# Two transformer blocks on one core: first norm by ones and logarithm, two modulation scales on TensorE, head 0's forget gate first, pool evictions ahead of weight splits

## The reference

```python
def first_block(x, c, norm_pre_w, ada_w, ada_b, w_in, ...):
    silu_c = silu(c)
    mod = silu_c @ ada_w + ada_b                 # 1024 -> 3072
    shift, scale, gate = split(mod, 3)
    h = rms_norm(x, norm_pre_w) * (1 + scale) + shift
    u_pool, g_pool, q, f_pre, i_in, g_h = split(h @ w_in, 6)   # 1024 each
    pool_out = multiscale_pool(u_pool, pool_w, pool_scale) * silu(g_pool)
    f = lb + (1 - lb) * sigmoid(f_pre)
    log_f = log(f); k = 1 - f                    # 8 heads of 128, chunks of 64
    o = hgrn2_chunkwise(q, log_f, k, i_in)
    o = rms_norm(o, hgrn_norm_w) * silu(g_h)
    y = concatenate([pool_out, o]) @ w_out
    return x + gate * rms_norm(y, norm_post_w)

def second_block(x, c, ctx, c_ctx, w_ada, b_ada, w_in, ...):
    x = layer_norm(x); ctx = layer_norm(ctx)
    mod = silu(c) @ w_ada + b_ada                # 1024 -> 6144
    ...                                          # latent attention, convolution, FFN
```

## Time and profile before

| | us |
|---|---|
| median of 3 runs | 1217.19 |
| profiled execution, its own time | 1213.69 |
| its span in the trace | 1211.9 |
| PE busy | 1133.1 (94%) |
| DVE busy | 860.9 (71%) |
| ACT busy | 550.8 (45%) |
| POOL (GpSimd) busy | 165.3 (14%) |

### The profile page before, as it was taken

How to read it: one execution, slowest core, us unless ns; L and a number is a source line. 1 busy time by engine, 2 the same in 40 slices (tenths; PEclk the granted TensorE clock), 3 DMA queues, 4 the chain that set the end, 5 groups by cost and what they waited for, 6 DMA issues and landing times.

```text
span 1211.9 us, 14076 instructions
## 1 busy us (share of the span) xinstructions
PE 1133.1 (94%) x5488; PEld 925.6 (76%) x5488; DVE 860.9 (71%) x1352; ACT 550.8 (45%) x851; POOL 165.3 (14%) x179
## 2 busy tenths in 40 slices
PE   1879999999999989989999999998999999999996
PEld 0667888888888868879887766777888888888885
DVE  5868899988876775455888899586666565655236
ACT  3266454545433242667334656545634434342230
POOL 0034433344424210001010010000000000000001
PEclk9989999999999999999999999999999999999999
DMA  7724133233344567472211011111322222234201
GB/s 295 296 106 154 70 140 139 74 136 132 111 148 165 182 220 171 178 66 84 96 50 47 1 70 45 60 56 49 104 105 104 105 76 99 104 115 173 80 33 69
DMA packets 28306, 136.59 MB, mean 113 GB/s; under 512 B 7760, under 2 KB 8016, under 8 KB 14416
## 3 DMA queue, kind: packets, MB, share of 16 engines
q1 hardware_dynamic: 20448, 128.46, 30.5%
q10 hardware_dynamic: 7792, 7.24, 2.4%
HBM read 133.57 MB, written 2.12 MB: 112 GB/s over the span
## 4 chain that ended last, share of the span: by engine, by line
PE 64%; DVE 18%; ACT 9%; DMA 4%; issue 3%; POOL 1%; ACTq 0%; DVEq 0%; SPq 0%
PE PB L185 63%; DVE RAW L1365 4%; ACT WH L199 3%; DMA RAW<-in_wstream 2%; ACT L200 2%; DVE WL L206 2%; DVE CV L214 2%; DVE XL L214 1%; DVE SS L214 1%; DMA vectors<-PX 1%; DVE HL L206 1%; DMA XL<-in_xT 1%; DVE HB L231 1%; PE PB L193 1%; POOL UPA L206 1%
## 5 line engine op out<-in xcount | busy, mean ns | idle before, releaser
L185 PE MATMUL PB<-HH,WH 128*128 128x512 f32 (+1 forms) x896 | 353.3, 394 | 18.5 <-DVE WL L206 8.0
L206 DVE TENSOR_TENSOR WL<-RAW,WH 128x1024 fp32r<-128x1024 f32 (+2 forms) x174 | 202.5, 1171 | 199.1 <-ACT WH L199 198.4
L185 PE MATMUL PB<-HH,WL 128*128 128x512 f32 (+1 forms) x896 | 342.7, 382 | 0.0
L185 PE MATMUL PB<-HL,WH 128*128 128x512 f32 (+1 forms) x896 | 342.4, 382 | 0.0
L199 ACT ACTIVATE WH<-RAW 128x1024 fp32r<-128x1024 f32 (+2 forms) x174 | 169.6, 981 | 296.5 <-PE PB L185 262.5
L185 PEld LDWEIGHTS PB<-HH,WH 128*128 128x128 f32 x896 | 171.1, 191 | 54.0 <-DVE WL L206 9.0
L185 PEld LDWEIGHTS PB<-HH,WL 128*128 128x128 f32 x896 | 170.7, 190 | 33.3
L185 PEld LDWEIGHTS PB<-HL,WH 128*128 128x128 f32 x896 | 171.2, 191 | 29.0 <-issue 0.5
L214 DVE SCALAR_TENSOR_TENSOR CV<-VP,PC,CV 128x512 f32<-128x512 f32 x120 | 86.7, 765 | 0.7
L206 POOL TENSOR_TENSOR PX<-PX,NPOW 128x2 f32<-128x2 f32 (+2 forms) x7 | 6.2, 893 | 482.0 <-DVE PX L206 436.1
L185 PE MATMUL PB<-WH,AH 128*128 128x512 f32 x176 | 68.5, 389 | 0.0
(11 more groups left out here) (270 smaller groups left out, 1851.9 us busy)
## 6 DMA issues: line engine op xcount, KB each, us to landing
RAW<-in_wstream SPq DMA_DIRECT2D x108, 1024.0 KB, 4.8
RAW<-in_wstream SPq DMA_DIRECT2D x5, 768.0 KB, 4.3
RAW<-in_wstream SPq DMA_DIRECT2D x5, 512.0 KB, 3.6
XL<-in_xT SPq DMA_DIRECT2D x2, 1024.0 KB, 8.2
HB<-in_x SPq DMA_DIRECT2D x2, 1024.0 KB, 6.3
out<-XL SPq DMA_DIRECT2D x8, 256.0 KB, 2.0
ROWS<-in_rows ACTq DMA_DIRECT2D x3, 512.0 KB, 7.7
XC<-in_ctx SPq DMA_DIRECT2D x1, 1024.0 KB, 7.1
```

What stands on the lines that cost most here:

```text
L185: return self.put(lambda e: e.matmul(o, l, r, start=start, stop=stop, skip_group_check=skip))
L206: return self.put(lambda e: e.tensor_tensor(o, a, b, op))
```

## The change

It makes these edits. The lengths of the stream's items stay as they are; one copy of c in columns (8) is added to the parameters.

1. c's row is loaded first on ACT's queue, its Silu comes before the squares, and c also stands in the parameters as columns.
2. The squares are summed in pairs on DVE and by three matmuls with all of `ONES` (512 columns each) on PE; ACT takes logarithm and exponential (-0.5) from PSUM to `Q0`. The power, the diagonals, the spread and the sum for `BX` go; the exponential for the lower bounds and its four small operations move behind the start.
3. The scale tiles of pairs 1 and 2 become items of kind "m", laid out for PE: 16 fp32 matmuls of one column each (`modulation`). They stand on PE before the first tiles and before the fifth.
4. Of head 0 the forget gate's block comes first in the last pair, and sigmoid, f, logarithm, k and scan of head 0 stand ahead of the other evictions and between the splits. Both dots of the first later item stand there too; the others of the plan stay where they are or move up, and in blocks 6, 10, 14, ... 30 they stand on ticks 2 and 3.
5. In `pool_mix` the eviction and both parts come ahead of the split of block nb+4.
6. The squares of x for the second block's layer norm are four dots of DVE in blocks 65 and 66.
7. The split of block 74 comes ahead of the last `y_squares` and `gated`.

```diff
 def stream_layout():
-    first = [("a", "ada_w", j + b) for j in range(0, 8, 2) for b in (8, 0)]
+    first = [("m" if b and j in (2, 4) else "a", "ada_w", j + b) for j in range(0, 8, 2) for b in (8, 0)]
 def dot_plan():
-    todo = [(n, i, vec) for n in LATER_ADA for i, vec in dots_of(n)]
+    todo = [(n, i, vec) for n in LATER_ADA[1:] for i, vec in dots_of(n)]
     for n, t in ticks:
-        if t % 2 and todo:
+        if (t >= 2 if n < B_POOL and n % 4 == 2 else t % 2) and todo:
 # sp_prog, fetch
+                elif LAY[n - NRAW][0] == "m":
+                    sp.wait_ge(S_.p_sm, ("mod", (LAY[n - NRAW][2] - 8) // 2))
 # pool_prog
-        g.wait_ge(S_.v_ax, "xs")
-        power(sct(2)[:, 4:8], sct(2)[:, 0:4], 4, "xpow")
 # act_prog, start
+        a.dma(ROW["c"], A["rows"][:, 0:D]).then_inc(S_.cs, "c", by=16)
         a.dma(PC[:, :], A["params"][:, :]).then_inc(S_.par, "par", by=16)
...
+        a.wait_ge(S_.cs, "c")
+        a.act(ROW["c"], ROW["c"], ACTF.Silu).then_inc(S_.a_s, "c")
         a.wait_ge(S_.par, "par")
-        a.dma(ROW["c"], A["rows"][:, 0:D]).then_inc(S_.cs, "c", by=16)
-        a.act(LT, LT, ACTF.Exp).then_inc(S_.a_s, "lt")
+        a.act(col("c", 0, 8), col("c", 0, 8), ACTF.Silu).then_inc(S_.a_s, "ccol")
         for k in range(8):
             a.act(XSQ[k], XT[:, k, :], ACTF.Square).then_inc(S_.a_s, ("xsq", k))
+        a.act(Q0[:, :], aux.of("xs"), ACTF.Ln, bias=NPOW[:, 7:8], scale=1.0 / D).then_inc(S_.a_ax, "xs")
+        a.act(Q0[:, :], Q0[:, :], ACTF.Exp, scale=-0.5).then_inc(S_.a_s, "xd")
+        a.act(LT, LT, ACTF.Exp).then_inc(S_.a_s, "lt")
 # act_prog, head 0
-        for b in range(4):
-            split(b + NW)
-        for b in range(3):
-            head(0, b)
+        a.wait_ge(S_.p_blk, 1)
+        a.act(Kb, main.of(("z", 0, 1)), ACTF.Sigmoid).then_inc(S_.a_ev, ("z", 0, 1))
+        split(NW)
+        a.wait_ge(S_.v_s, ("f", 0))
+        a.act(XR[3], Kb, ACTF.Ln).then_inc(S_.a_s, ("ln", 0))
+        head(0, 0)
+        split(NW + 1)
+        head(0, 2)
+        split(NW + 2)
+        split(NW + 3)
 # act_prog, pool_mix (DVE alike)
-            after(nb)
             kk = 2 * p + m
             mix(kk, GPS[p % 2][:, m, :], (S_.v_ev if p else S_.v_ax, ("pm", p, m)), None if kk >= 2 else (S_.p_blk, 53))
+            split(nb + NW)
 # act_prog, seam (DVE alike, ahead of gated(3, 1))
         shifted(1)
+        split(B_IN2 + 2)
         y_squares(2, 1)
 # dve_prog, start
-        for k in range(1, 8):
+        for k in (1, 2, 3):
             v.tt(Q0[:, :], Q0[:, :], XSQ[k], ADD).then_inc(S_.v_s, ("xs", k))
-        v.ts(BX, aux.of("xs")[:, 0:4], 1.0 / D, EPS2, MUL, ADD)
-        v.ts(sct(2)[:, 0:4], aux.of("xs")[:, 0:4], 1.0 / D, EPS1, MUL, ADD).then_inc(S_.v_ax, "xs")
-        diag(DG, sct(2)[:, 4:8], 4, "xd")
+        for k in (4, 6):
+            v.tt(XSQ[k], XSQ[k], XSQ[k + 1], ADD).then_inc(S_.v_s, ("xs", k))
         for p in range(4):
...
+            if p in FIRST_MOD:
+                v.wait_ge(S_.p_sm, ("mod", p))
+                v.tt(M1[:, 8 + 2 * p:10 + 2 * p], aux.of(("mod", p))[:, 0:2], col("ada_b", 8 + 2 * p, 2), ADD)\
+                    .then_inc(S_.v_ax, ("mod", p))
...
-                v.stt(XT[:, k, :], XT[:, k, :], A1[:, k:k + 1], aux.of("xd"), MUL, MUL)\
-                    .then_inc(S_.v_s, ("u", k), *["xd"] * (k == 7))
+                v.stt(XT[:, k, :], XT[:, k, :], A1[:, k:k + 1], Q0[:, :], MUL, MUL).then_inc(S_.v_s, ("u", k))
 # dve_prog, head 0: OML, LT, LB, OML (moved here), then
+        dot(first, 0, "c")
+        v.ts(Kb, Kb, OML[:, 0:1], LB[:, 0:1], MUL, ADD).then_inc(S_.v_s, ("f", 0))
+        split(NW)
+        dot(first, 1, "c")
+        v.ts(Kb, Kb, -1.0, 1.0, MUL, ADD).then_inc(S_.v_s, ("k", 0))
+        v.scan(Bb, SM[:, :], XR[3]).then_inc(S_.v_s, ("b", 0))
+        for n in (1, 2, 3):
+            split(NW + n)
 # dve_prog, blocks 65 and 66
+                for i in ((0, 1) if nb == B_OUT + 11 else (2, 3)):
+                    v.dot(XSQ2, XT2[:, i, :], XT2[:, i, :], MUL, BX[:, i:i + 1], scale=1.0 / D).then_inc(S_.v_st, ("bx", i))
 # pe_prog
-        sums(bk, Q0, 4, 0).then_inc(S_.p_sm, "xs")
-        spread("xd", DG, 4, "xd")
+        for n, k in enumerate((3, 4, 6)):
+            pe.wait_ge(S_.v_s, ("xs", k))
+            op = pe.mm(bk, ONES[:, :], XSQ[k] if n else Q0[:, :], n == 0, n == 2)
+        op.then_inc(S_.p_sm, "xs")
+        def modulation(p):
+            n = FIRST_MOD[p]
+            bk = take_aux(("mod", p), 1 + p)
+            pe.wait_ge(S_.raw[n % NRAW], n)
+            pe.wait_ge(S_.a_s, "ccol")
+            for i in range(2):
+                for k in range(8):
+                    op = pe.mm(bk[:, i:i + 1], raw_of(n)[:, D * i + 128 * k:D * i + 128 * k + 128], col("c", k), k == 0, k == 7)
+            op.then_inc(S_.p_sm, ("mod", p))
+        modulation(1)
...
         for b in range(2):
             for k in range(2):
                 first_tile(b, k)
+        modulation(2)
...
-        for p in (2, 3):
-            for b in range(4):
+        for p, bs in ((2, range(4)), (3, (1, 0, 2, 3))):
+            for b in bs:
```

More of the change, by code:

```diff
@@ L268 @@
 for n_, it_ in enumerate(LAY):
-    if it_[0] == "a":
+    if it_[0] in ("a", "m"):
         size_ = 2048
@@ L279 @@
 NRAW, NW = 3, 4
+FIRST_MOD = {(it[2] - 8) // 2: n for n, it in enumerate(LAY) if it[0] == "m"}
 FIRST_ADA = [n for n, it in enumerate(LAY) if it[0] == "a" and it[1] == "ada_w" and it[2] < 16]
@@ L856, in act_prog @@
             a.act(XSQ[k], XT[:, k, :], ACTF.Square).then_inc(S_.a_s, ("xsq", k))
-        a.wait_ge(S_.cs, "c")
-        a.act(ROW["c"], ROW["c"], ACTF.Silu).then_inc(S_.a_s, "c")
+        a.wait_ge(S_.p_sm, "xs")
+        a.wait_ge(S_.g_s, "npow")
+        a.act(Q0[:, :], aux.of("xs"), ACTF.Ln, bias=NPOW[:, 7:8], scale=1.0 / D).then_inc(S_.a_ax, "xs")
+        a.wait_ge(S_.a_ax, "xs")
+        a.act(Q0[:, :], Q0[:, :], ACTF.Exp, scale=-0.5).then_inc(S_.a_s, "xd")
+        a.wait_ge(S_.v_s, "lt")
+        a.act(LT, LT, ACTF.Exp).then_inc(S_.a_s, "lt")
         def h_high(k):
@@ L1398, in dve_prog @@
             v.tt(Q0[:, :], Q0[:, :], XSQ[k], ADD).then_inc(S_.v_s, ("xs", k))
-        v.wait_ge(S_.p_sm, "xs")
-        v.ts(BX, aux.of("xs")[:, 0:4], 1.0 / D, EPS2, MUL, ADD)
-        v.ts(sct(2)[:, 0:4], aux.of("xs")[:, 0:4], 1.0 / D, EPS1, MUL, ADD).then_inc(S_.v_ax, "xs")
-        v.wait_ge(S_.g_s, "xpow")
-        v.wait_ge(S_.idn, "idn")
-        diag(DG, sct(2)[:, 4:8], 4, "xd")
+        for k in (4, 6):
+            v.wait_ge(S_.a_s, ("xsq", k + 1))
+            v.tt(XSQ[k], XSQ[k], XSQ[k + 1], ADD).then_inc(S_.v_s, ("xs", k))
         for p in range(4):
-            for n in FIRST_ADA[2 * p:2 * p + 2]:
-                for i, vec in dots_of(n):
-                    dot(n, i, vec)
+            for n in FIRST_ADA:
+                if LAY[n][2] % 8 == 2 * p:
+                    for i, vec in dots_of(n):
+                        dot(n, i, vec)
             ks = slice(2 * p, 2 * p + 2)
+            if p in FIRST_MOD:
+                v.wait_ge(S_.p_sm, ("mod", p))
+                v.tt(M1[:, 8 + 2 * p:10 + 2 * p], aux.of(("mod", p))[:, 0:2], col("ada_b", 8 + 2 * p, 2), ADD)\
+                    .then_inc(S_.v_ax, ("mod", p))
+                v.wait_ge(S_.v_ax, ("mod", p))
             v.wait_ge(S_.v_ada, ("ada_w", 2 * p + 1, "c"))
@@ L1504, in hgrn @@
                     .then_inc(S_.v_ax, ("dg", h))
-        for b in range(4):
-            split(b + NW)
-        for b in range(4):
-            head(0, b)
+        v.wait_ge(S_.a_s, "lt")
+        v.recip(OML, LT).then_inc(S_.v_s)
+        v.wait_ge(S_.v_s)
+        v.tt(LT, LT, OML, MUL).then_inc(S_.v_s)
+        v.wait_ge(S_.v_s)
+        v.tt(LB, LT, LT, SUB).then_inc(S_.v_s)
+        v.wait_ge(S_.v_s)
+        v.ts(OML, LB, -1.0, 1.0, MUL, ADD).then_inc(S_.v_s, "lb")
+        first = LATER_ADA[0]
+        dot(first, 0, "c")
+        Vb, Kb, Bb, Qb, Gb = head_bufs(0)
+        v.wait_ge(S_.a_ev, ("z", 0, 1))
+        v.wait_ge(S_.v_s, "lb")
+        v.ts(Kb, Kb, OML[:, 0:1], LB[:, 0:1], MUL, ADD).then_inc(S_.v_s, ("f", 0))
+        split(NW)
+        dot(first, 1, "c")
+        v.wait_ge(S_.a_s, ("ln", 0))
+        v.ts(Kb, Kb, -1.0, 1.0, MUL, ADD).then_inc(S_.v_s, ("k", 0))
+        v.wait_ge(S_.msk, "m")
+        v.scan(Bb, SM[:, :], XR[3]).then_inc(S_.v_s, ("b", 0))
+        for n in (1, 2, 3):
+            split(NW + n)
         for step in range(-6, 0):
@@ L1534, in pool_mix @@
         def pool_mix(p, m, nb):
-            after(nb)
+            v.wait_ge(S_.p_blk, nb)
             kk = 2 * p + m
@@ L1683, in dve_prog @@
         x1(1)
+        split(B_IN2 + 2)
         gated(3, 1)
-        split(B_IN2 + 2)
         split(B_IN2 + 3)
@@ L2524, in host_layout @@
             continue
+        if it[0] == "m":
+            a = np.asarray(inputs[it[1]])[0]
+            parts.append(np.concatenate([a[:, 128 * j:128 * j + 128].reshape(8, 128, 128).transpose(1, 0, 2).reshape(128, D)
```

(2 more changed lines are left out.)

33 lines of the change are left out of this document (13 added, 20 removed), and 2 rows, old and new, of the table PARAMS.

## The result

The kernel after takes 1203.9 us (median of 4 runs, 1202.2 to 1206.9), the kernel before on the same chip 1216.7. The ratio is 0.9885 with a 95% interval of 0.9858 to 0.9912: faster by 0.9 to 1.4%, some 13 us, where 24.6 were forecast; 1203.9 lies just above the range. The profiled execution took 1202.2 us (span 1200.4; before 1213.7 and 1211.9): its own gain is 11.5.

What follows compares the result with a forecast made beforehand. PE was busy 94% of the span, so time was PE's work plus its waits and the low clock behind them. 2.6 + 9.4 + 4.6 + 5.5 + 2.5 = 24.6 off 1217.2 gave 1192.6 us, range 1184 to 1203.

Steps and rivals of the forecast that it cites:

- A: The start through the first 32 tiles: first scaling at 20.7, tiles' end at 60.0, 2.6 us gained.
- T: The end of the first 32 tiles on PE: 62.6 us in the kernel before, forecast 60.0.
- PE's products become the first stage's chain: Rival, chance 0.22: low clock and gaps end the first 32 tiles at 63.5, 0.9 later than before; 1196.1 us.
- B: From the first 32 tiles' end to 97 us: 6.2 of idle and 3.2 of low clock saved, 9.4 us.
- The scan at T+1: Sign of being right: head 0's scan starts from T+1, where before it started 5.8 behind T.
- the clock's share: From T to 97 us: of three low-clock stretches one is kept, 3.2 us saved.
- The 3.64 goes: PE's 3.64 us wait at 92.80, for block 8's late weights, goes as the buffer is refilled some 20 us earlier.
- C: Heads, six waits for the chain of SS: 3.6 us from waits and 1.0 for the low stretch at 250.5, 4.6 us.
- D: Pooling: PE's 3.84 us wait at 444.57 and the low stretch behind it go, 5.5 us.
- The split of block 56 still waits for its weights, but PE needs it at 451.: Pooling step: block 56's split waits for its weights, yet is ready before PE needs it at 451 us.
- E: Second stage: block 74's split earlier gains 1.6 us, plus half the low stretch there, 2.5 us.
- the shortened waits come back as others: Rival, chance 0.13: head 0's exponentials behind four splits and late splits in pooling; 12 us gained, 1205 us.

Runs made afterwards that it cites:

- mod2_vec_masks: mod2_vec with the loads of masks, SM and FAC also issued behind ACT's squares: 1201.3 us, ratio 0.9854 to the kernel before.
- scales_dve: Kernel after with both middle scale groups back on DVE's dots, their one-column products on PE gone: 1198.3 us, ratio 0.9814 to the kernel before.
- scales_vec: Kernel after with both middle scale groups back on DVE and the four scattered stores behind the next split: 1201.2 us, ratio 0.984 to the kernel before.
- ada0_back: Kernel after with the first later item's two dots back in the heads' ticks: 1205.9 us, ratio 0.9896 to the kernel before.
- scan_last: Kernel after with DVE's splits of the first head's three other blocks ahead of the scan: 1202.2 us, ratio 0.9863 to the kernel before.
- head0_back: Kernel after with the first head's blocks in their old order, the first later item's dots still early: 1205.9 us, ratio 0.9889 to the kernel before.
- ticks_back: Kernel after with the output block's dots back on their old ticks in the heads: 1208.6 us (10 runs), ratio 0.992 to the kernel before.
- g1_late: Kernel after with ACT's wait for the scattered gate vector, and its two row loads, moved from block 56 to 60: 1204.3 us, ratio 0.9866 to the kernel before.
- mod2_vec: Kernel after with only the second middle scale group on TensorE and the four scattered stores behind the next split: 1204.9 us, ratio 0.9881 to the kernel before.
- pool_back: Kernel after with the old pooling order, splits ahead of evictions and products: ratio 0.989 to the kernel before (four runs, 1203.1 to 1212.1 us).

## Why the prediction was right in sign and too large

**A, 2.6 forecast, 1.3 found** (T 61.26, forecast 60.0). First scaling 1.2 late, most of it x's landing (1.9 later than before, not 0.9). That was put down to c's row alone; mod2_vec_masks, with c's row as early but the masks late, has x at 11.24, so it takes both to hold it back. The table load took the 1.28 of the sum: the exponential starts 1.31 us behind the logarithm's end, with no drain to see. The 2.66 that the Trainium skill ("ScalarE: Activation LUTs", What ACT_TABLE_LOAD costs) gives a switch with a drain isn't borne out here. The Trainium skill's section on table sets has one set with both functions, yet here too a load stands between them. The step that failed in judgement is the one that called moving scales to PE part of a gain: scales_dve and scales_vec, with no such products, have T at 58.97 and 58.57, the eight programs with them at 61.2 on average. So the rival "PE's products become the first stage's chain" had the mechanism, with a smaller price than its 3.5.

**B, 9.4 forecast, 5.4 found: the term most mis-sized** (4.7 from 64 to 97 us, and the 0.7 of the wait right behind T). The scan at T+1 came true, and so did the clock's share, 3.2 forecast: three low stretches became one. The idle saved was put at 6.2 and is 2.4: PE idles 6.5 us from T on, not 2.6. "The 3.64 goes" is true, but not all of it was gain: ada0_back has only 1.98 there, 1.8 us of lead. And the waits in front, put at 2.6 in all, were 0.9, 2.9 and 2.6. POOL's work on the earlier scan runs beside DVE's splits and takes 6.99 us instead of 3.95 (scan_last); without that the waits are one of 5.17, so POOL's slowness alone isn't the reason, and what else holds them isn't settled. That the order of the first head brings the rest isn't borne out: head0_back has no less of it.

**C, 4.6 forecast, 3.4 found.** That DVE holds the heads back is right: period 36.08 (35.9 forecast), with waits for AT in place of those for SS. The low stretch at 250.5 did go. ticks_back puts the edit's worth at 4 us by the runs, with intervals that overlap, and more by its one profile.

**D, 5.5 forecast, 4.9 found at 450 us, 0.8 left at 490, nothing at 530.** The step that failed: "The split of block 56 still waits for its weights, but PE needs it at 451." It waits for the scattered store's landing, in ACT's order, until 461.39, and PE, now earlier, needs the split before that. g1_late shows it, and shows the next ones behind it: XC's load at 485 and the four stores' issue at 511.

**E, 2.5 forecast, 2.5 found** between 530 and 545 us: the low stretch at 544.1 is gone, and the waits there are 0.95 and 0.80 instead of 0.69 and 2.04. No run takes this edit out, nor the four dots of edit 6. The kernel before also had low stretches at 789.9, 834.3 and 1206.3 us, beyond the six places that the prediction counts; the one near 775 in the kernel after is 6.8 us long instead of 3.4, and takes 1.0 later.

Together, by the leads (2.0 at 64 us is A with the first 0.7 of B): 2.0 + 4.7 + 3.4 + 4.8 - 4.1 - 0.8 + 2.5 - 1.0 = 11.5. Of the 13.1 missing, 4.0 are B, 1.3 A, and 4.9 what pooling gave back. It is the rival "the shortened waits come back as others" (0.13, 1205) that came nearest, and I gave it too little. Its number fits better than its terms: it had B at 4 and D at 2 for splits late in pooling, where B was 5.4 and pooling's gain went to the store in ACT's queue. I had sought late splits in pooling on their weights' load and on evictions and not on what else stands in that queue.

From 490 to 530 the lead rises by 0.9 in the four kernels with the stores late; in the others it goes from 0.3 up to 8.4 down. Take 0.9, less the PE waits there, less 1.7 for each 3.4 us of low clock behind them: all nine others come out within 0.6 us. Why such a wait is 1.2 us in one kernel and 3.6 in another isn't settled.

## What to carry to other kernels

- Before counting a removed wait as gained, list for the next 50 us everything that the engines do *in order* ahead of what PE will ask for: transfers awaited for another purpose, and DMA issues themselves. If one of them ends at a fixed time, PE's being early turns into a wait there, and a low stretch behind it may take what was left.
- Moving work to the engine that waits is a gain only if its data is there during the wait. Here the item landed as the wait ended, and the products then ran at the low clock on the chain (mod2_vec: T 63.3, after 61.26).
- One profile per variant has a spread of 2 us by its first 64 us alone, and once of 5; compare the rise of the lead over the stage that an edit touches, not the end, and count the low stretches in it before you call the rest the edit's.

## What the runs showed of the hardware that I had not expected

- POOL beside DVE: six subtractions on tiles of 128x256 take 6.99 us while DVE runs splits of 1.2 us and goes straight on (after), 3.94 where DVE idles 1.96 us and then multiplies tiles of 128x256 (scan_last). Same operations, same kernel but for the order.
- A store of 1024 scattered numbers takes 11.4 to 14.5 us to land in all runs at this place (four in a row, up to 22.1), and a 1 MB stream load issued beside it, behind another one, 12.2 instead of 4.9 us (after, 449.77 against 463.74). Its issue takes 0.39 alone; in the row of four it went up to 3.02 (pool_back) and 4.27 (ticks_back).
- The granted clock of the profile's windows doesn't tell all at the start: in after, 24.3 to 31.3 us has 1.00, yet 32 one-column passes take 6.99 us there, exactly what they take in mod2_vec at a granted 0.50. The pace has to be read from the durations until the first low stretch is on record.
